# Sample and prompt memory keys transposed by VectorE, 32 by 32, ahead of the attention that reads them

## The reference

```python
hm = rmsnorm(mem, norm_mem)
mk = (hm @ w_ck).reshape(bsz, n_mem, X_HEADS, X_HEAD_DIM)
...
qx = (h2 @ w_cq).reshape(bsz, t_len, X_HEADS, X_HEAD_DIM)
scores = jnp.einsum('bthd,bmhd->bhtm', qx, mem_k).astype(jnp.float32) * (X_HEAD_DIM ** -0.5)
probs = jax.nn.softmax(scores, axis=-1).astype(x.dtype)
ctx = jnp.einsum('bhtm,bmhd->bthd', probs, mem_v).reshape(bsz, t_len, D_MODEL)
```

## Time and profile before

| | |
|---|---|
| median of 3 runs | 1666.66 us (1665.84 to 1668.19) |
| span of the profiled execution, first to last instruction | 1663.2 us |
| its own time beside the span | not listed; the median lies 3.5 us above the span |
| PE, DVE, ACT, POOL busy | 99%, 58%, 40%, 11% |
| DMA | 229.79 MB, mean 138 GB/s over the span |
| TensorE clock granted, mean | 0.998 |

### The profile page before, as it was taken

How to read it: one execution, slowest core, us unless ns; L and a number is a source line. 1 busy time by engine, 2 the same in 40 slices (tenths; PEclk the granted TensorE clock), 3 DMA queues, 4 the chain that set the end, 5 groups by cost and what they waited for, 6 DMA issues and landing times.

```text
span 1663.2 us, 31696 instructions
## 1 busy us (share of the span) xinstructions
PE 1643.0 (99%) x12906; PEld 1522.8 (92%) x12906; DVE 969.9 (58%) x1676; ACT 673.3 (40%) x1146; POOL 183.7 (11%) x191
## 2 busy tenths in 40 slices
PE   7999999999999999999999999999999999999998
PEld 5887899999999999999999999999999987499998
DVE  5776446665756647565433343333887753499952
ACT  5566345254442543435322222222343333344542
POOL 0121001111121112111100001111000000001120
PEclk9999999999999999999999999999999999999999
DMA  7898734243232432333333334444223399733462
GB/s 266 261 295 254 219 92 119 55 109 99 70 99 53 115 91 77 91 84 96 101 81 83 86 104 139 132 132 138 62 87 97 98 388 396 229 103 105 126 187 108
DMA packets 277534, 229.79 MB, mean 138 GB/s; under 512 B 10825, under 2 KB 244178, under 8 KB 271970
## 3 DMA queue, kind: packets, MB, share of 16 engines
q1 hardware_dynamic: 277184, 228.42, 44.9%
q10 hardware_dynamic: 258, 0.09, 0.0%
HBM read 201.31 MB, written 27.53 MB: 138 GB/s over the span
## 4 chain that ended last, share of the span: by engine, by line
PE 92%; DVE 4%; issue 1%; ACT 1%; DMA 1%; POOL 0%; SPq 0%; DVEq 0%; ACTq 0%; POOLq 0%
PE pj L287 48%; PE pj L486 10%; PE pj L2203 7%; PE dk L2203 5%; PE pj L2946 2%; PE dk L2515 2%; PE pj L2539 1%; PE dk L2439 1%; PE dk L1819 1%; PE pj L2450 1%; PE pj L2548 1%; PE dk L1272 1%; PE dk L1278 1%; PE dk L825 1%; PE dk L2975 1%
## 5 line engine op out<-in xcount | busy, mean ns | idle before, releaser
L287 PE MATMUL pj<-a_hi,w_high 128*128 128x272 f32 x1792 | 394.1, 301 | 0.0
L287 PE MATMUL pj<-a_hi,w_low 128*128 128x272 f32 x1792 | 370.4, 288 | 0.0
L287 PE MATMUL pj<-a_lo,w_high 128*128 128x272 f32 x1792 | 369.7, 288 | 0.0
L287 PEld LDWEIGHTS pj<-a_hi,w_high 128*128 128x128 f32 x1792 | 280.9, 189 | 13.4 <-issue 8.1
L271 DVE TENSOR_TENSOR w_low<-w_raw,w_high 128x2048 fp32r<-128x2048 f32 x76 | 173.9, 2288 | 192.7 <-ACT w_high L261 192.6
L287 PEld LDWEIGHTS pj<-a_lo,w_high 128*128 128x128 f32 x1792 | 281.6, 189 | 0.0
L287 PEld LDWEIGHTS pj<-a_hi,w_low 128*128 128x128 f32 x1792 | 280.1, 189 | 0.1
L261 ACT ACTIVATE w_high<-w_raw 128x2048 fp32r<-128x2048 f32 x76 | 145.4, 1913 | 57.9 <-PE pj L287 45.9
L2087 ACT ACTIVATE q_high<-q_part 128x512 fp32r<-128x512 f32 x140 | 77.5, 620 | 73.3 <-DVE q_part L2141 37.0
L287 PE MATMUL pj<-mix_hi,w_high 128*128 128x272 f32 x512 | 105.9, 288 | 0.0
L287 PE MATMUL pj<-mix_lo,w_high 128*128 128x272 f32 x512 | 105.5, 288 | 0.0
(11 more groups left out here) (482 smaller groups left out, 3029.5 us busy)
## 6 DMA issues: line engine op xcount, KB each, us to landing
w_raw<-in_w_in_dram SPq DMA_DIRECT2D x48, 1024.0 KB, 5.9
w_raw_wide<-in_w_ck_dram SPq DMA_DIRECT2D x16, 1024.0 KB, 8.6
w_raw_wide<-in_w_cv_dram SPq DMA_DIRECT2D x16, 1024.0 KB, 7.9
w_raw<-in_w_out_dram SPq DMA_DIRECT2D x16, 1024.0 KB, 6.0
q_part<-in_w_cq_dram SPq DMA_DIRECT2D x48, 256.0 KB, 3.6
w_raw<-in_w_co_dram SPq DMA_DIRECT2D x8, 1024.0 KB, 8.3
q_part<-in_w_co_dram SPq DMA_DIRECT2D x32, 256.0 KB, 3.8
xr<-xT_scratch SPq DMA_DIRECT2D x16, 272.0 KB, 6.3
```

The lines of the kernel that those rows point to most:

```text
L287: mm = pe.matmul(pj[:, 2 * (q % 2) + b, 0:n], wt[:, k, :], x(k, o, n), start=(k == 0 and m == 0), stop=(k == KT - 1 and m == 2))
```

## The change

A new scratch `keysT_d` in memory takes the sample keys with the width on the partitions. During the pool stage, and then the output stage, VectorE makes it in units. A unit of the pool stage is half a sample (1 MB): `keys_in` loads it with 4 DMAs, each into 32 partitions; `keys_turn` turns it in 32x32 blocks in two instructions; `keys_out` stores it with 8 DMAs, each from 32 partitions. There are 10 such units (one for each tile from group 1 on, stored and turned a tile later), all in one buffer `kin` and two `kout`, which lie where `mix_hi` 6 to 15 do not. The other 3 samples go through 12 units of half that size in the output stage. The low end of `mix_hi` (rows 0 to 5) may be written only when all ten units are stored, so `MIX_PARTS` is reordered and the first tile of the output stage waits for that part. PE no longer turns sample keys, ACT and DVE no longer copy them, and the attention's order of work and of loads is written anew. The prompt keys are turned in the opening by DVE, from `mst` straight to `kts`, and stored by 4 DMAs per group in runs of 256 bytes; their tokens come out in another order, which the exponentials' access pattern undoes.

```diff
+        keysT_d = nc.dram_tensor("keysT_scratch", [NB, P, KT, MEM], F32, kind="Internal").ap()
...
+                        for i in range(4):
+                            dst = kT_d[4 * j - 4:4 * j, :, i * 2 * T32:(i + 1) * 2 * T32].rearrange("k (b p) r -> p (k b) r", p=T32)
+                            sp.dma_start(dst, kts[i * T32:(i + 1) * T32].rearrange("p n m r -> p n (m r)")).then_inc(kts_stored, 16)
...
-                    if 1 <= j <= KEY_GROUPS and 1 <= q <= 2:
-                        steps[6] = [turn_keys(j - 1, q - 1)]
...
+                    if 1 <= j <= KEY_GROUPS and 1 <= q <= 2:
+                        dve.wait_ge(pj_read, 4 * j)
+                        at_least(dve, kts_stored, 64 * (j - 1))
+                        dve.transpose(kts[:, :, q - 1, :], mst[:, q - 1, :].rearrange("p (n d) -> p n d", d=T32)).then_inc(kts_ready, 1)
...
+        POOL_UNITS = 10
+        OUT_UNITS = 12
...
+        def keys_in(sp, dst, b, first, loaded):
+
+            for i in range(4):
+                cols = slice(first + i * dst.shape[-1], first + (i + 1) * dst.shape[-1])
+                src = t["cache_mem_k"][0, b].rearrange("(g m) h d -> m g (h d)", m=T32)
+                sp.dma_start(dst[i * T32:(i + 1) * T32], src[:, :, cols]).then_inc(loaded.sem, 16)
+
+        def keys_out(sp, src, b, tile, step, first, n, stored):
+
+            for i in range(4):
+                dst = keysT_d[b, first * T32:(first + n) * T32, tile + step * i, :].rearrange("(j d) m -> d j m", d=T32)
+                sp.dma_start(dst, src[i * T32:(i + 1) * T32].rearrange("p j g m -> p j (g m)")).then_inc(stored.sem, 16)
...
+        def keys_turn(dve, dst, src):
+
+            return dve.transpose(dst[:].rearrange("p j g m -> p g j m"), src.rearrange("p g (j d) -> p g j d", d=T32))
+
+        def sp_keys(sp, n):
+
+            if 0 < n <= POOL_UNITS:
+                sp.wait_ge(k_turned.sem, k_turned.at(2 * n))
+                for f in range(2):
+                    keys_out(sp, kout[f], (n - 1) // 2, 8 * ((n - 1) % 2) + f, 2, 0, 4, k_stored[f])
+            if n < POOL_UNITS:
+                if n == 0:
+                    sp.wait_ge(oa_done, HEADS)
+                keys_in(sp, kin, n // 2, 8 * P * (n % 2), k_in_loaded)
+
+        def dve_keys(dve, n):
+
+            if 0 < n <= POOL_UNITS:
+                dve.wait_ge(k_in_loaded.sem, k_in_loaded.at(64 * n))
+                for f in range(2):
+                    at_least(dve, k_stored[f], 64 * (n - 1))
+                    keys_turn(dve, kout[f], kin[:, :, f * P:(f + 1) * P]).then_inc(k_turned.sem, 1)
...
+                    if not first:
+                        sp_keys(sp, 4 * (g - 1) + q)
...
+                    if g == 3 and q == 3:
+                        mix_take_high(act, 3)
...
-        MIX_PARTS = ((0, 4), (4, 8), (8, 14), (14, 16))
+        MIX_PARTS = ((6, 8), (8, 12), (12, 14), (0, 6), (14, 16))
...
             if m == 3:
+                for s in k_stored:
+                    act.wait_ge(s.sem, s.at(64 * POOL_UNITS))
+                act.wait_ge(k_turned.sem, k_turned.at(2 * POOL_UNITS))
...
+                        if g == 3:
+                            mix_take_low(dve, 3)
                         dve_windows(dve, g, 0)
+                    if g > 0:
+                        dve_keys(dve, 4 * (g - 1) + q)
...
+        def sp_keys_late(sp, i):
+
+            if 1 < i <= OUT_UNITS + 1:
+                sp.wait_ge(k_late_turned.sem, k_late_turned.at(2 * (i - 1)))
+                b, h = divmod(2 * POOL_UNITS + i - 2, XH)
+                for f in range(2):
+                    keys_out(sp, kout_late[f], b, 4 * h, 1, 2 * f, 2, k_late_stored[f])
+            if 0 < i <= OUT_UNITS:
+                if i == 1:
+                    sp.wait_ge(k_turned.sem, k_turned.at(2 * POOL_UNITS))
+                b, h = divmod(2 * POOL_UNITS + i - 1, XH)
+                keys_in(sp, kin_late, b, h * XD, k_late_loaded)
...
+            sp_ktb(sp, 0)
+            load_keys(sp, 0, 0, 8)
+            load_keys(sp, 0, 8, KT)
+            load_keys(sp, 1, 0, 12)
+            load_keys(sp, 1, 12, KT)
+            sp_ktb(sp, 1)
+            load_keys(sp, 2, 0, 8)
+            load_keys(sp, 3, 0, 8)
...
+        KEYS_AT = (("w", 1), ("raw_a", 1), ("hi_end", 1), ("lo_end", 1), ("raw_b", 1), ("high", 1), ("w", 2), ("raw_a", 2))
+        VALUES_AT = (("hi_end", 2), ("lo_end", 2), ("raw_b", 2), ("high", 2), ("w", 3), ("q_a", 1), ("q_b", 1), ("raw_b", 3))
...
             sp_vtb(sp, 0)
+            for b in (2, 3):
+                load_keys(sp, b, 8, KT)
+            for b in (4, 5):
+                load_keys(sp, b, 0, 8)
+                load_keys(sp, b, 8, KT)
             sp_vtb(sp, 1)
+            sp.wait_ge(sc_done.sem, sc_done.at(1))
+            sp_ktb(sp, 2)
+            for b, scored in ((6, 1), (7, 2)):
+                sp.wait_ge(sk_done.sem, sk_done.at(scored))
+                load_keys(sp, b, 0, 8)
+                load_keys(sp, b, 8, KT)
+            sp.wait_ge(sc_done.sem, sc_done.at(2))
+            sp_ktb(sp, 3)
             sp.wait_ge(cx_done.sem, cx_done.at(4))
             sp_vtb(sp, 2)
+            for b, scored in ((0, 3), (1, 4)):
+                sp.wait_ge(sk_done.sem, sk_done.at(scored))
+                load_values(sp, b)
             sp.wait_ge(cx_done.sem, cx_done.at(8))
             sp_vtb(sp, 3)
+            for b, scored in ((2, 5), (3, 6), (4, 7)):
+                sp.wait_ge(sk_done.sem, sk_done.at(scored))
+                load_values(sp, b)
+            sp.wait_ge(sk_done.sem, sk_done.at(NB))
+            sp.dma_start(raw[0][:], source("co", 0, 0)).then_inc(w_loaded[0], 16)
+            sp.wait_ge(sc_done.sem, sc_done.at(XH))
+            load_values(sp, 5)
+            load_values(sp, 6)
+            sp.wait_ge(sv_done.sem, sv_done.at(3))
+            load_values(sp, 7)
+            sp.dma_start(raw[1][:], source("co", 0, 1)).then_inc(w_loaded[1], 16)
+            sp.wait_ge(sv_done.sem, sv_done.at(NB))
             sp.dma_start(raw[2][:], source("co", 0, 2)).then_inc(w_loaded[2], 16)
...
+            def scores(b):
+
+                loaded(pe, b, KEYS_AT)
+                pe.wait_ge(qm_ready.sem, qm_ready.at(b + 1))
+                for d in range(DT):
+                    for h in range(XH):
+                        mm = pe.matmul(pj[h * NS:(h + 1) * NS, 0, 0:MEM], qmb[b % 2][:, DT * h + d, :],
+                                       kept_keys[KEYS_AT[b][0]][:, DT * h + d, :],
+                                       start=(b == 0 and d == 0), stop=(b == NB - 1 and d == DT - 1))
+                mm.then_inc(sk_done.sem, 1)
...
             every = range(DT)
+            pe.wait_ge(col2_root, 1)
+            pe_prompt_scores(pe, 0)
+            pe.wait_ge(rest_out.sem, rest_out.at(7 * PAIRS))
+            scores(0)
+            scores(1)
             pe_prompt_scores(pe, 1)
+            turn(0)
+            context(0, every)
+            scores(2)
+            scores(3)
+            turn(1)
+            context(1, every)
+            scores(4)
+            pe_prompt_scores(pe, 2)
+            for b in (5, 6, 7):
+                scores(b)
+            pe_prompt_scores(pe, 3)
...
             turn(2)
-            values(4)
-            values(5)
+            for b in (0, 1, 2):
+                values(b)
             context(2, every)
+            turn(3)
+            for b in (3, 4, 5):
+                values(b)
             values(6)
-            turn(3)
```

More of the change, by code:

```diff
@@ L1928, in body @@
                                              ALU.mult, ALU.subtract).then_inc(h_low, 1)
-            body(0)
-            with dve.Fori(1, 4) as j:
+            for j in range(4):
                 body(j)
```

339 lines of the change are left out of this document (145 added, 194 removed).

## The result

| | before | after |
|---|---|---|
| median | 1666.74 us (1665.41 to 1668.19, 13 runs) | 1671.67 us (1668.02 to 1673.58, 13 runs) |
| span of the profiled execution | 1663.2 us | 1671.8 us |
| ratio of the medians | | 1.0026, 95% interval 1.0019 to 1.0033 |

The prediction, 1648.7 us in a range of 1638 to 1667 and 81% for faster, was wrong: the kernel is slower. The span of before lay 3.5 us under the median of its runs, and that of after at its own; the profiled execution of after was the slowest of the 13 (1673.58 us).

A forecast was written before the change was run, and what follows sets the result against it. PE, busy 99% of the span, was taken as the bound, with transfers close behind in opening and attention. 1663.2 - 25 - 3 + 10 = 1645.2 us of span, plus 3.5 us, gave 1648.7 us; range 1638 to 1667.

The forecast's parts named there:

- the term of the pool stage, "+10": Pool stage: serial chain of ten units makes the map start at 986.9, 10 us lost, mostly PE waiting before output.
- The price of a packet: Pool stage: a 1 KB packet of a 32-partition DMA was taken to cost 78 ns, with 45 and 90 as ends.
- my own formula: Pool stage: a unit's period is 128 packets times their price plus 4.2 us; at 78 ns, 14.2 us.
- no sharing: Rival for 1 KB packets in the pool stage: 45 ns each, 0 to 1 us lost, 1639 to 1641 us; chance 0.22.
- SP's list is delayed too, but weights are three tiles ahead: Pool stage: SP waits for each turn before the next weight load, but weights are three tiles (39 us) ahead.
- The sign that I gave: End of pool stage: PE waits 5 to 8 us before the first output tile and again before the map.
- Attention, -25: Attention: PE loses 27.9 us of transposes; the stage ends at 1437.7 instead of 1462.3, gaining 25 us, bounds 20 to 28.
- The two limits meet: Attention: the stage would end at 1436.9 by PE and at 1437.7 by transfers.
- Opening, -3: Opening: PE loses 8 turns, 3.5 us, and DVE hides its added transposes; 3 us gained, bounds +3.5 and -5.
- The stores in 256-byte runs, my worry: Opening: 128 packets per queue and group cost 1.8 us below, 3.5 to 7 us above, against 1.4 us before.
- Output stage, 0: Output stage: half-size units fit in a 12 us tile and cost nothing; without that cover, 1 to 2 us a unit.
- slower, by the serial chain of units: Rival, pool stage: gains of 28 used up at 93 ns a packet, period 16.1 us; slower from 96 ns; chance 0.12.

## Why the prediction was wrong

**The step that failed** is the term of the pool stage, "+10": it was +28. Its chain, step by step, ends 19.3 us behind the predicted 986.9. The first turn ended at 838.03 instead of 836.6, 1.4 us. Nine periods of 15.83 instead of 14.2 are 14.7. And from the last turn (980.5) to the map it took 25.7 us instead of 22.5: I had let the second set of window sums follow the first at once, but between them ACT refills `ux`, POOL copies it and PE turns it, and PE's last 30 products of the tile took 5.77 us, at a granted clock of 0.60 from 1000 to 1006 us, instead of 3.75.

**The price of a packet**, inside that term, was between the bounds but not where I put it. By my own formula the period is 14.7 at the measured 82 ns and 15.7 at 90; it was 15.83. So only 0.5 of the 1.6 us that a period ran over is the packets' price, and 1.1 us, 10 over nine periods, is something for which the formula has no term. What it is stays open. The DMA lines above show two candidates: the queues run nearly empty for 0.6 us (slices 1 to 4) between a unit's stores and the bulk of its loads, and the weight tile's 512-byte packets mix with the last of the loads, so that from 849 us on few of the unit's packets are left and its turn still starts only at 851.27. I had weighed "no sharing" (0.22) more than the upper end, and had set aside the estimate by the 189 GB/s of the Trainium skill, SBUF — State Buffer, Door 1: The DMA port swizzle (a period of 15.3 us and a loss of 20). That estimate came nearer to the period than mine, but in part by luck: its packet, 11.1 us for 128 of them or 87 ns, is as far above the measured one as my 78 is below. Wide loads alone gave back 20.3 us, so it is shown that narrow DMAs make the loss. "The stores' first packets were not yet in each other's way" was a reason to choose by, and no row bore it.

**"SP's list is delayed too, but weights are three tiles ahead"** is the sentence that missed a second limit. It is true of the weight tiles. `pw` is not three tiles ahead: SP issues it in the first tile of a group, and PE wants it in the second. Behind twelve DMAs of a unit, one weight tile and an issue that itself takes 6.5 us it came late, 16.2 us in all, nearly all of them in two groups. It cost the total little only because the units' chain was late as well (2.6 us when mended alone). The sign that I gave, 5 to 8 us of waiting before the first output tile and again before the map, did not come: at the end of the stage PE stood 1.9 us before the first output product and 3.2 before the turn of `ucol`.

**The cast of rows 0 to 5** was counted behind the last unit and nowhere else. It costs 4.4 us without any unit, and nearly all of that by the low part ahead of the window sums: moved behind them the map ends 3.1 us earlier (4.1 when both are counted from the start of the head stage, 210.51 and 211.46 us).

**Attention, -25**, was right in its mechanism and 3.6 us too large. The last values landed 87.2 us behind the stage's start instead of 85.7, with an issue of 7.58 us ahead of them, and what PE does behind them took 11.0 us instead of 9.4: PE had been busy only 1.07 of the 4 us before, and its first 16 products took 3.36 us at a granted clock of 0.56, against 1.85. "The two limits meet" was too kind: the loads are the limit, at a share of 1.00.

**Opening, -3**, was nothing: 0.3 later in the run of the opening alone, 0.8 in the whole change. Even these are within chance: with the old opening the head stage starts at 210.51 us in before and at 211.10 in the run with the sample keys alone. PE lost the 3.5 us of turns and waits 3.2 us for `xts`. "DVE is busy 38 of 50 us there and hides them" reasons from a mean share; DVE's transposes stood in front of what PE waits for next. The stores in 256-byte runs, my worry, did no harm: `kts` landed after 4.0 us in the run of the opening alone, and there from 69 to 70 us 1090 packets, nearly all of 256 bytes, carry 0.29 MB, 15 ns each over 16 queues. That is the lower bound of the term; the upper one, a full 512-byte packet (28 ns) to twice that, did not come.

**Output stage, 0**, holds: the long run of products behind the pool stage's map takes 198.04 us before and 198.03 after.

**Smaller slips** of the working moved nothing: reading in the earlier trace rows picks up in the second slice, from 1333.7 us, and not in the third; and by the prediction's own 1.22 us per ns, with no more than the 10 us of the pool stage to win back, packets of 65 to 84 ns are 1639 to 1656 us instead of 1643 to 1655, and 92 ns is 1666 instead of 1663.

**The sum** was then 1663.2 - 21.4 + 0.8 + 28.1 + 0.8 = 1671.5. The rival that came true, "slower, by the serial chain of units" (0.12), named the place and the mechanism. Its point, a period of 16.1 us, was set against gains of 28; the gains were 21, so a period of 15.8 sufficed.

## What to carry to other kernels

When work is added to a queue, list every transfer behind it with its own slack, and not only the large ones: the smallest load of the stage, issued one tile ahead, was the first to be late. When two things are late at once, mending either alone shows almost nothing (6.1 and 2.6 us), and the pair shows nearly all (18.9 of 22.4); so look at the waits again after each mend instead of dropping the edit. And a DMA's shape has two prices, the partitions it touches and its outermost count: the first cost 22.5 us here, more than the 21.4 that the attention gained, and the second 144. Mended in this way, and with the old opening, the change makes the kernel 1.2% faster than before instead of 0.26% slower.

## What the chip showed that I had not expected

- A DMA confined to 32 partitions moves 1 KB packets at some 200 GB/s, and over 128 partitions faster: landing falls from 5.9 to 4.0 us for the loads of 256 KB, and a weight tile behind them from 10.4 to 8.4.
- A DMA with an outermost count of 4 runs at a quarter of the DMA share, some 90 GB/s: the kernel takes 1815.4 us instead of 1671.7.
- The issue of a DMA takes 0.3 to 0.5 us, but 6.5 us behind thirteen DMAs with 3 MB issued in the 6 us before, and 7.6 in the attention. It holds back SP's whole list, so that everything behind it is issued late.
- A stall costs more than its length, by the granted clock. The stretches around the first wait for `pw`, columns as in the earlier trace rows:

```profile
878.00:881.00 3.00, 3.00 (x26) 3.00 (x25) 0.00 (x0) 2.28 (x2) 0.00 (x0) 1.00 1.15 203
...
884.00:887.00 3.00, 0.00 (x0) 0.00 (x0) 3.00 (x3) 0.00 (x0) 0.00 (x0) 0.72 0.69 168
887.00:890.00 3.00, 1.24 (x3) 1.01 (x4) 0.65 (x1) 0.00 (x0) 0.00 (x0) 0.50 0.86 243
...
893.00:896.00 3.00, 3.00 (x21) 2.77 (x21) 1.48 (x2) 0.00 (x0) 0.00 (x0) 1.00 0.91 199
```

PE, busy at 2.4 GHz until then, stands from 882.4 to 888.8 us. The clock falls to 0.50, its level of 1.2 GHz, while it stands, is still there when the map begins, and is back at 1.00 from 893 on. The map's 16 products take 5.61 us there, against 3.83 for the same map in the kernel before, so the stand of 6.3 us costs 8.1.
